# Other SBUF addresses for the operands of the products of a two-block model kernel

## The kernel before

| tensors | before |
|---|---|
| `x`, `h_hi`, `h_lo` | 128 |
| `w_raw`, `w_hi`, `w_lo`, `w_first`, `ada_raw`, `consts`, `s_b` | 128 |
| `ones_r`, `half_r` | 64 |
| T tiles (`hx`, `v_stage`, `rstd`, gelu, tanh, ...), `blocks` | 128 |
| all of the last region: `v`, `y_*`, `ada_up`, `h_full`, `hk_*`, `yb_*`, `m_*`, `k_t`, `v_b`, `qk`, `xg_*`, `gu_*`, `p_t`, `wf_*`, `q_n` (most), `ws_t` | 192 |

## Time and profile before

### The profile page before, as it was taken

The page is one execution under the profiler, slowest core; times in us unless marked ns, Lnnn a source line. Parts: engine busy times, 40 slices in busy tenths (PEclk is TensorE's granted clock), DMA queues, the critical chain, the costliest instruction groups (busy, mean ns, idle before and its releaser), DMA issues.

```text
span 1432.1 us, 19800 instructions
## 1 busy us (share of the span) xinstructions
PE 1409.6 (98%) x7326; PEld 1173.2 (82%) x7326; DVE 991.7 (69%) x1529; ACT 649.3 (45%) x1046; POOL 48.3 (3%) x47
## 2 busy tenths in 40 slices
PE   8999999999999999999999999999899999999999
PEld 6998888888889888888887877776688888888887
DVE  7966777778898688888887788988675344323333
ACT  5743333332366665656644666675443232221221
POOL 0001000001100000000001000000030000000000
PEclk9999999999999999999999999999999999999999
DMA  9994444466722211221113221120032222322222
GB/s 376 379 362 181 177 176 176 176 244 270 284 83 90 89 59 60 69 79 59 59 59 118 90 88 60 41 78 31 30 118 73 103 88 90 115 88 88 96 87 81
DMA packets 35327, 181.41 MB, mean 127 GB/s; under 512 B 4153, under 2 KB 4921, under 8 KB 20930
## 3 DMA queue, kind: packets, MB, share of 16 engines
q1 hardware_dynamic: 34050, 177.95, 33.6%
q10 hardware_dynamic: 1216, 2.64, 0.6%
HBM read 177.94 MB, written 2.11 MB: 126 GB/s over the span
## 4 chain that ended last, share of the span: by engine, by line
PE 90%; DVE 7%; ACT 2%; issue 1%; DMA 0%; ACTq 0%; DVEq 0%
PE acc L1703 79%; PE ada L1703 4%; PE turn L1703 3%; PE norm L1703 2%; DVE w_lo L976 1%; PE turn L2136 1%; DVE s L969 1%; PE turn L1997 1%; DVE stat L1545 1%; DVE hx L969 1%; DVE hk_lo L969 0%; ACT w_hi L544 0%; DVE z_t L1318 0%; DVE s_b L969 0%; ACT hk_hi L568 0%
## 5 line engine op out<-in xcount | busy, mean ns | idle before, releaser
L1703 PE MATMUL acc<-h_hi,w_hi 128*128 128x512 f32 x984 | 390.4, 397 | 1.1 <-DVE rstd L969 1.0
L1703 PE MATMUL acc<-h_hi,w_lo 128*128 128x512 f32 x984 | 384.4, 391 | 0.0
L1703 PE MATMUL acc<-h_lo,w_hi 128*128 128x512 f32 x984 | 383.9, 390 | 0.0
L976 DVE TENSOR_TENSOR w_lo<-w_raw,w_hi 128x2048 fp32r<-128x2048 f32 (+1 forms) x106 | 245.6, 2317 | 66.0 <-ACT w_hi L544 65.9
L544 ACT ACTIVATE w_hi<-w_raw 128x2048 fp32r<-128x2048 f32 (+1 forms) x106 | 200.8, 1895 | 122.8 <-PE acc L1703 122.0
L1703 PEld LDWEIGHTS acc<-h_hi,w_lo 128*128 128x128 f32 x984 | 185.1, 188 | 39.9
L1703 PEld LDWEIGHTS acc<-h_hi,w_hi 128*128 128x128 f32 x984 | 185.4, 188 | 39.4 <-DVE w_lo L976 1.4
L1703 PEld LDWEIGHTS acc<-h_lo,w_hi 128*128 128x128 f32 x984 | 185.3, 188 | 37.3 <-issue 0.2
L1703 PE MATMUL acc<-w_hi,h_hi 128*128 128x256 f32 x320 | 91.6, 287 | 0.7 <-DVE w_lo L976 0.7
L969 DVE SCALAR_TENSOR_TENSOR x<-acc,mods,x 128x512 f32<-128x512 f32 (+1 forms) x40 | 33.0, 828 | 83.9 <-PE acc L1703 83.9
L1703 PE MATMUL acc<-w_lo,h_hi 128*128 128x256 f32 x320 | 90.2, 283 | 0.0
(11 more groups left out here) (302 smaller groups left out, 2511.6 us busy)
## 6 DMA issues: line engine op xcount, KB each, us to landing
w_raw<-in_weights SPq DMA_DIRECT2D x102, 1024.0 KB, 4.8
ada_v<-in_ada SPq DMA_DIRECT2D x32, 512.0 KB, 6.2
ada_raw<-in_ada SPq DMA_DIRECT2D x32, 512.0 KB, 5.7
ada_out<-in_ada SPq DMA_DIRECT2D x32, 512.0 KB, 6.4
ada_up<-in_ada_first SPq DMA_DIRECT2D x8, 1024.0 KB, 17.2
w_raw<-in_weights SPq DMA_DIRECT2D x4, 768.0 KB, 4.0
x<-in_x SPq DMA_DIRECT2D x2, 1024.0 KB, 6.1
w_first<-in_weights SPq DMA_DIRECT2D x4, 512.0 KB, 13.6
```

Of the source, the lines that this page charges most:

```text
L976: nc.vector.tensor_tensor(w_lo[par][:, 0:used], w_raw[par][:, 0:used], f32(w_hi[par][:, 0:used]), ALU.subtract)\
L1703: return nc.tensor.matmul(out, lhsT, rhs, start=start, stop=stop)
```

## The change

Only addresses change; no instruction is added, removed or moved, and no wait. `place(rest)` skips up to the next address that is `rest` modulo 256, some small tensors are rounded to 32 bytes instead of 64 to make room, and the last region has four bases: `big`, `early = big + 64`, `mid = up = big + 128`.

```diff
-    def take(nbytes):
+    def take(nbytes, step=64):
         off = top[0]
-        top[0] += (nbytes + 63) // 64 * 64
+        top[0] += (nbytes + step - 1) // step * step
         return off
+
+    def place(rest):
+        top[0] += (rest - top[0]) % 256
...
     h_lo = at("h_lo", [P, KT, TOK], off_h + 16 * KB, F32R)
+    place(192)
     w_raw = [at(f"w_raw{s}", [P, 2048], take(8 * KB)) for s in range(2)]
...
     c_col = at("c_col", [P, TB, 8], take(128))
+    place(0)
     sh_pair = at("sh_pair", [P, KT, 2], take(64), F32R)
...
     off_blocks = take(4 * (8 * P + 4))
+    place(96)
     big = top[0]
-    v = at("v", [P, TB, AW], big)
-    y_lo = at("y_lo", [P, TB, AW], big, F32R)
-    y_hi = at("y_hi", [P, AT, TOK], big + 32 * KB, F32R)
+    early, mid, up = big + 64, big + 128, big + 128
+    v = at("v", [P, TB, AW], early)
+    y_lo = at("y_lo", [P, TB, AW], early, F32R)
+    y_hi = at("y_hi", [P, AT, TOK], early + 32 * KB, F32R)
...
-    hk_hi = at("hk_hi", [P, KT, TOK], big + 24 * KB, F32R)
-    hk_lo = at("hk_lo", [P, KT, TOK], big + 40 * KB, F32R)
-    yb_hi = at("yb_hi", [P, QH, TOK], big + 24 * KB, F32R)
+    hk_hi = at("hk_hi", [P, KT, TOK], mid + 24 * KB, F32R)
+    hk_lo = at("hk_lo", [P, KT, TOK], mid + 40 * KB, F32R)
+    yb_hi = at("yb_hi", [P, QH, TOK], mid + 24 * KB, F32R)
...
-    m_hi = at("m_hi", [P, KT, TOK], big + 24 * KB, F32R)
+    m_hi = at("m_hi", [P, KT, TOK], mid + 24 * KB, F32R)
...
     xg_hi = at("xg_hi", [P, KT, TOK], big, F32R)
     gu_hi = at("gu_hi", [P, FF1, TOK], big, F32R)
     gu_lo = at("gu_lo", [P, FF1, TOK], big + 32 * KB, F32R)
```

More of the change, by code:

```diff
@@ L138, in program @@
     mods = at("mods", [P, NMOD], take(4 * NMOD))
-    gains = at("gains", [P, 8], take(32))
-    gscale = at("gscale", [P, 8], take(32))
+    gains = at("gains", [P, 8], take(32, 32))
+    gscale = at("gscale", [P, 8], take(32, 32))
     off_rstd = take(2 * KB)
@@ L148, in program @@
     row_part = at("row_part", [P, 2, 8], take(64))
[L149 to L153, removed]
+    row_max, row_sum, row_inv, row_weight = [at(f"row_{name}", [P, 8], take(32, 32)) for name in ("max", "sum", "inv", "weight")]
+    stat2 = at("stat2", [P, 3, 2, 2], take(64, 32))
+    lam_inv = at("lam_inv", [P, 2], take(8, 32))
+    lam_two = at("lam_two", [P, 2], take(8, 32))
+    neg_lam = at("neg_lam", [P, 1], take(4, 32))
     c_col = at("c_col", [P, TB, 8], take(128))
+    place(0)
     sh_pair = at("sh_pair", [P, KT, 2], take(64), F32R)
-    w_shift = at("w_shift", [P, 2], take(8))
-    bf_col = at("bf_col", [8, 1], take(4))
+    w_shift = at("w_shift", [P, 2], take(8, 32))
+    bf_col = at("bf_col", [8, 1], take(4, 32))
     wf_raw = at("wf_raw", [P, KT, 8], take(256))
@@ L160, in program @@
     half_r = at("half_r", [P, P], take(4 * P), F32R)
-    eps_tile = at("eps_tile", [P, 1], take(4))
+    eps_tile = at("eps_tile", [P, 1], take(4, 32))
     ident, ones = consts[:, K_ID:K_ID + P], ones_r[:, :].bitcast(F32)
@@ L176, in program @@
     off_blocks = take(4 * (8 * P + 4))
+    place(96)
     big = top[0]
-    v = at("v", [P, TB, AW], big)
-    y_lo = at("y_lo", [P, TB, AW], big, F32R)
-    y_hi = at("y_hi", [P, AT, TOK], big + 32 * KB, F32R)
[L182 to L188, removed]
+    early, mid, up = big + 64, big + 128, big + 128
+    v = at("v", [P, TB, AW], early)
+    y_lo = at("y_lo", [P, TB, AW], early, F32R)
+    y_hi = at("y_hi", [P, AT, TOK], early + 32 * KB, F32R)
+    ada_up = [at(f"ada_up{s}", [P, 2, DM], early + 8 * KB * s) for s in range(UP)]
+    ada_v = [at(f"ada_v{s}", [P, DM], early + 32 * KB + 4 * KB * s) for s in range(4)]
+    x_n = at("x_n", [P, KT, TOK], early + 48 * KB)
+    h_full = at("h_full", [P, KT, TOK], early + 48 * KB)
+    csil = [at("csil0", [P, DM], up + 68 * KB), at("csil1", [P, DM], T[0])]
+    ws_t = at("ws_t", [P, GROUPS, P], up + 64 * KB)
+    ada_out = [at(f"ada_out{s}", [P, DM], off) for s, off in enumerate((off_ada, off_ada + 4 * KB, up + 64 * KB, up + 68 * KB))]
     b_sp = at("b_sp", [P, GROUPS, P], off_blocks)
@@ L198, in program @@
     v_b = at("v_b", [P, TB, NKV * P], big + 12 * KB)
-    hk_hi = at("hk_hi", [P, KT, TOK], big + 24 * KB, F32R)
-    hk_lo = at("hk_lo", [P, KT, TOK], big + 40 * KB, F32R)
-    yb_hi = at("yb_hi", [P, QH, TOK], big + 24 * KB, F32R)
-    yb_lo = at("yb_lo", [P, QH, TOK], big + 40 * KB, F32R)
-    q_n = [[at(f"q_n{s}_{n}", [P, TOK], (big + 68 * KB, off_rstd, T[1])[n] if s == 0 else big + (56 + 2 * n) * KB) for n in range(3)]
+    hk_hi = at("hk_hi", [P, KT, TOK], mid + 24 * KB, F32R)
+    hk_lo = at("hk_lo", [P, KT, TOK], mid + 40 * KB, F32R)
+    yb_hi = at("yb_hi", [P, QH, TOK], mid + 24 * KB, F32R)
+    yb_lo = at("yb_lo", [P, QH, TOK], mid + 40 * KB, F32R)
+    q_n = [[at(f"q_n{s}_{n}", [P, TOK], (up + 68 * KB, off_rstd, T[1])[n] if s == 0 else up + (56 + 2 * n) * KB) for n in range(3)]
            for s in range(2)]
@@ L206, in program @@
     s_b = [at(f"s_b{c}", [P, TOK], off_ada + 2 * KB * c) for c in range(4)]
-    p_t = [at(f"p_t{c}", [P, TOK], big + (62 + 2 * c) * KB) for c in range(2)]
+    p_t = [at(f"p_t{c}", [P, TOK], up + (62 + 2 * c) * KB) for c in range(2)]
     z_b = [at("z_b0", [P, TOK], T[2]), at("z_b1", [P, TOK], T[5])]
-    sq_hi_k = [at(f"sq_hi_k{s}", [P, TOK], big + (56 + 2 * s) * KB, F32R) for s in range(2)]
-    sq_lo_k = [at(f"sq_lo_k{s}", [P, TOK], big + (60 + 2 * s) * KB, F32R) for s in range(2)]
-    sq_hi_q, sq_lo_q = at("sq_hi_q", [P, TOK], big + 66 * KB, F32R), at("sq_lo_q", [P, TOK], big + 70 * KB, F32R)
+    sq_hi_k = [at(f"sq_hi_k{s}", [P, TOK], up + (56 + 2 * s) * KB, F32R) for s in range(2)]
+    sq_lo_k = [at(f"sq_lo_k{s}", [P, TOK], up + (60 + 2 * s) * KB, F32R) for s in range(2)]
+    sq_hi_q, sq_lo_q = at("sq_hi_q", [P, TOK], up + 66 * KB, F32R), at("sq_lo_q", [P, TOK], up + 70 * KB, F32R)
     z_t = at("z_t", [P, TOK], T[7])
@@ L221, in program @@
     v_2 = [at(f"v2{s}", [P, TB, 2 * P], big + (16 + 4 * s) * KB) for s in range(2)]
-    m_hi = at("m_hi", [P, KT, TOK], big + 24 * KB, F32R)
-    m_lo = at("m_lo", [P, KT, TOK], big + 40 * KB, F32R)
-    c_rows = [at(f"c_rows{kind}", [P, 4, TOK], big + (24 + 16 * kind) * KB) for kind in range(2)]
+    m_hi = at("m_hi", [P, KT, TOK], mid + 24 * KB, F32R)
+    m_lo = at("m_lo", [P, KT, TOK], mid + 40 * KB, F32R)
+    c_rows = [at(f"c_rows{kind}", [P, 4, TOK], mid + (24 + 16 * kind) * KB) for kind in range(2)]
     c_row = [c_rows[n % 2][:, n // 2, :] for n in range(8)]
     cum_dram = nc.dram_tensor("cum_rows", (8, TOK), F32, kind="Internal").ap()
-    sq_hi_2, sq_lo_2 = at("sq_hi_2", [P, TOK], T[2], F32R), at("sq_lo_2", [P, TOK], big + 70 * KB, F32R)
-    s_2 = [at(f"s_2{s}", [P, 2, TOK], off) for s, off in enumerate((big + 56 * KB, big + 60 * KB, off_blocks))]
-    pt_2 = [at(f"pt_2{s}", [P, TOK], big + 64 * KB + 2 * KB * s) for s in range(3)]
+    sq_hi_2, sq_lo_2 = at("sq_hi_2", [P, TOK], T[2], F32R), at("sq_lo_2", [P, TOK], up + 70 * KB, F32R)
+    s_2 = [at(f"s_2{s}", [P, 2, TOK], off) for s, off in enumerate((up + 56 * KB, up + 60 * KB, off_blocks))]
+    pt_2 = [at(f"pt_2{s}", [P, TOK], up + 64 * KB + 2 * KB * s) for s in range(3)]
     lam_rows = at("lam_rows", [P, 256], T[8])
     lam_prod = at("lam_prod", [P, 128], T[8] + KB)
-    wf_hi = at("wf_hi", [P, KT, P], big + 56 * KB, F32R)
-    wf_lo = at("wf_lo", [P, KT, P], big + 60 * KB, F32R)
+    wf_hi = at("wf_hi", [P, KT, P], up + 56 * KB, F32R)
+    wf_lo = at("wf_lo", [P, KT, P], up + 60 * KB, F32R)
     gate_abs = at("gate_abs", [8, TOK], T[5])
@@ L242, in program @@
     d_out = at("d_out", [P, TOK], T[7])
-    assert big + 72 * KB <= 229344, big
+    assert up + 72 * KB <= 229344, up
     pre = [at(f"pre{s}", [P, TOK], off_ada + 2 * KB * s) for s in range(3)]
     xg_hi = at("xg_hi", [P, KT, TOK], big, F32R)
-    xg_lo = [at(f"xg_lo{m}", [P, TOK], big + (16 + 2 * m if m < 4 else 56 + 2 * m) * KB, F32R) for m in range(KT)]
+    xg_lo = [at(f"xg_lo{m}", [P, TOK], big + (16 + 2 * m) * KB if m < 4 else up + (56 + 2 * m) * KB, F32R) for m in range(KT)]
     gu_hi = at("gu_hi", [P, FF1, TOK], big, F32R)
```

## The result

The changed kernel takes 1455.33 us (median of 4 runs, 1452.56 to 1458.03) against 1435.04 us before (4 runs, 1434.59 to 1437.33): ratio 1.0139, 95% interval 1.012 to 1.0159. It is slower by 20 us, where 1416 us was forecast. The profiled execution took 1452.56 us with a span of 1450.3 us, 18.2 us over that of before.

A forecast was written before the change was run, and what follows sets the result against it. PE's stream of products, through the spacing from one start to the next, was taken as the bound. The terms -16.7 - 2.0 - 0.5 - 2.2 + 1.9 + 0.8 = -18.7 us gave 1416 us, range 1392 to 1450.

The forecast's parts named there:

- The rule of two independent read ports: Skill's rule on TensorE's moving and weight reads: addresses don't matter, sum 0, 1435 us; 12%, effects that cancel included.
- Step 1: `columns` with h, 2952 products, distance 0 to +64: 220.6 ns, -6.3 ns each, -18.6 us, of which -16.7 us kept.
- nine tenths: Share of the gain on `columns` with h taken as kept, since DVE is busy in the attention stretches: -16.7 of -18.6 us.
- The floor: Lower bound for 512-column products: 216.7 ns, the spacing of plain float32 products with 256 columns at +64.
- step 7: 128 `w_first` products, plain float32 attention products, xg, DVE and ACT operations: 0, with 2 us either way for the others.
- the floor's rival: All 512-column products reach 216.7 ns: -41.4 us, 1393 us; 8%.
- Steps 2 to 4: `columns` with y, with hk, yb and m, and with gu: 223.8, 227.9 and 224.8 ns; -2.0, -0.5 and -2.2 us.
- Step 5: `rows` with h, 960 products, distance 0 to -64: 2.0 ns more each, +1.9 us.
- Step 6: `rows` with hk, 240 products, distance +64 to +32: +3.2 ns each, +0.8 us.
- The first rival: Settled +64 is slow: `columns` with h at 233.3 ns, +18.9 us; in all +22.8 us, 1458 us; 15%.
- step 3: `columns` with hk, yb and m, 480 products, distance -64 to -32: 227.9 ns, -1.0 each, -0.5 us.

The follow-up runs named there:

- sweep: Products alone, no model work, all 64 pairs of 8 addresses of h and 8 of w: columns 226.7 ns at distance 0, up to 234.3 at +96.
- last192: The changed kernel with the whole last region back at 192 modulo 256, where w is: 1446.14 us, ratio 1.0076 to the kernel before.
- base64: The kernel before with every address 64 bytes lower, all distances kept: 1435.69 us, ratio 1.0008.
- entry: Products alone, streams at other distances each followed by 96 products: all eight of rows at +64 took 113.3 ns, all of columns at 0 took 226.7.
- fine: Products alone, w in steps of 4 bytes with h at 0, then columns with 128 to 512 moving columns at five distances: lowest 226.7 ns at 512.

## Why the prediction was wrong

- **What bounds the kernel** was right: PE's stream of products. Nearly all of the change of spacing went into the time (+18.5 us of spacings, 18.2 of span), and the chain took no new engine in.
- **That addresses move the spacing, through the distance, was right** (sweep, last192, base64), though for rows at +64 the distance leaves two spacings open (entry). The rule of two independent read ports, by which the time should have stayed, failed. The Trainium skill states it in TensorE: Matmul & The Clock Gate, "Step-by-step: what each phase is for"; in sweep nothing runs but products and their weight loads, and the same pair of operands takes 226.7 or 234.3 ns by its distance alone. So the time of a product does depend on the two reads together; what it is in the chip that couples them, no run shows.
- **Step 1 failed**, in what it took +64 to cost. It held that a distance costs a 512-column product as much as a 256-column one, as the weight load lies beside the first part of either. fine shows the opposite: from d = 0 to +64 a product gains 6.7 ns at 256 columns and loses 6.7 ns at 512. The step forecast -6.3 ns and got +6.6 on 2952 products: +15.6 us where it had -16.7. Its own 6.3 ns had some luck in it: six of the sweep's eight stretches of rows at +64 run at 117.8 ns, 2.2 under d = 0. It had the right number at hand: the three products of the earlier trace rows at 233 ns were d = +64 with 512 columns, and were put aside as not settled. 233.3 ns is what such a stream settles at. The doubt was fair (in entry the first nine `columns` after a change of distance take 224 to 236 ns each), but 220.6 ns had no row at all. The argument from length (the load lies beside the first 1024 bytes) was an assumption about a mechanism; the row was a measurement of the very case. Why the length matters stays open.
- **Its nine tenths** were near the size that was seen (eight tenths), for a reason that holds in part. The sum is +15.6 us where 2952 x 6.6 would be 19.5. Some 2.5 us of the missing 3.9 are no wait: before, the interrupted streams of the attention stretches didn't settle and ran at 228 to 230 ns on average; after, they run at 233.3 as everywhere, so there was less to lose. Some 1.2 us lie in the 90 or so spacings above 245 ns, most of them with a wait or a dip of the clock inside: they sum to 33.3 us before and 32.1 after. There a slower PE waits less, as the step said the other way round.
- **The floor** of 216.7 ns was never approached: 226.7 is the lowest settled spacing of 512 columns in any run. Its rows are misread besides. The code has 64 products `w_first,h_full` and the trace 128 MATMULs (the x2 of the earlier trace rows): a plain float32 product is two MATMULs of some 217 ns, not one, and takes some 433 ns for 256 columns. The same holds for step 7's "128 products". No sum rests on it but those of the ends and of the floor's rival.
- **Steps 2 to 4** put unknown distances halfway between known ones (223.8, 227.9 and 224.8 ns). They are 233.3, 233.3 and 234.3: in steps of 32 bytes the spacing is no slope in d but lies between 232.4 and 234.3, with low places at 0 (226.7) and -64 (228.8).
- **Step 5** had the wrong sign: rows with h at -64 take 117.8 ns, not 122 (-1.7 us). It moved a number from 512 columns to 256, the same fault the other way round. **Step 6** was right in sign and small: 118.3 where 116.5 was taken, +1.1 us. It counted 240 products where there are 288; the page has 48 of them under another result tile.
- **Step 7** holds: `w_first` stays at its floor (sum -0.2 us), and the operations of DVE and ACT are as long as before (w_lo 2316 against 2317 ns on average).
- **The first rival** had the main term right: 233.3 ns with h and 1458 us; measured 233.3 and 1455.33. That the whole came so near has luck in it: it had +18.9 us for h (+15.6 seen), +1.7 for y and gu (+4.5), -0.5 for step 3 (+2.0) and +1.9 for rows with h (-1.7). It had 15% and lay outside the range.

## What to carry to other kernels

In a kernel bound by float32r products with 512 moving columns and a weight load for each, place the stationary operand at the same address modulo 256 as the moving one: 3% of the product's time hangs on it, and every other distance in steps of 32 bytes is worse. The kernel before had d = 0 for its largest group already, so bringing the others there gave 0.1%. Measure a distance with the product's own length: the order of distances at 256 columns is not that at 512. And where the trace holds even three products of the very case, give them at least the weight of a neat argument from a neighbouring one.

## What was not expected

- A product of 128 moving columns takes as long as one of 192: 111.7 ns, at all five distances.
- At one length the excess jumps: 448 columns at d = 0 have 20.0 ns over columns/2.4 where 384 and 512 have 13.3.
- The MATMULs of plain float32 products (`k_t,q_n`, `p_t,v_b`, `w_first,h_full`) kept their median spacing to 1 ns (112, 112 and 216) with their distances changed, so the effect was seen in float32r only. The first two stand at the 112 ns that short float32r products have at any distance, so only `w_first`, at one pair of distances, speaks for that.
- A stream can have two steady spacings at one distance (rows at +64: 113.3 and 117.8 ns).
- Several settled spacings are multiples of 6.67 ns: 113.3, 120, 226.7, 233.3; others aren't (117.8, 118.3, 228.8, 232.4, 234.3). What in the chip makes the spacing depend on the distance was not found.
